# Alternating the order of TensorE's threads by array tile in the recurrence stage of a two-block network

## The reference, cut to what matters

```
for d in range(2):        # RWKV-7 branch: 16 heads of 64, state (64, 64) per head
    S_t = S_{t-1} diag(w_t) - (S_{t-1} kk_t) b_t^T + v_t k_t^T;   y_t = S_t r_t
for d in range(2):        # gated delta rule: 8 heads of 128, state (128, 128) per head
    a_mat = I + strict_lower(kb k^T * decay)          # one per chunk of 64 tokens
    u, w  = solve(a_mat, [v * beta, kb * exp(gc)])
    v_new = u - w S;  o = (q exp(gc)) S + attn v_new;  S = S * g_end + k_end^T v_new
```

## Time and profile before

| what | us |
|---|---|
| median of 3 runs | 3913.81 |
| lowest, highest | 3911.79, 3920.32 |
| span of the profiled execution | 3908.8 |
| stage B in it, first to last matmul | 985 |

### The profile page before, as it was taken

One profiled execution on the slowest core, in us unless ns is written; L12 is line 12 of the kernel. 1 busy time (PEld: TensorE's weight loads), 2 busy tenths in 40 slices (PEclk: granted clock), 3 DMA queues, 4 the chain that ended last, 5 costly groups with the idle time before them and its releaser, 6 DMA issues. The chain is left out here.

```text
span 3908.8 us, 85968 instructions
## 1 busy us (share of the span) xinstructions
PE 3701.0 (95%) x37216; PEld 3426.5 (88%) x37216; DVE 2097.1 (54%) x3808; ACT 1503.6 (38%) x2641; POOL 1661.9 (43%) x1195
## 2 busy tenths in 40 slices
PE   7899998899998999999979999999998999999998
PEld 6799988799997788888868888888888999999998
DVE  5435434434435776677766666666646553434343
ACT  4344434334444432332223333333334444435343
POOL 4455555455554553333321111111115566666664
PEclk9999998999999999999989999999998999999999
DMA  5355553345444777778610010000006545555553
GB/s 214 128 184 186 192 185 141 140 173 184 162 162 147 251 264 263 246 253 293 222 38 20 24 27 28 19 15 23 6 3 232 178 173 185 182 184 183 184 184 130
DMA packets 116392, 587.21 MB, mean 150 GB/s; under 512 B 20912, under 2 KB 40496, under 8 KB 51376
## 3 DMA queue, kind: packets, MB, share of 16 engines
q1 hardware_dynamic: 116016, 581.71, 41.9%
HBM read 560.95 MB, written 20.71 MB: 149 GB/s over the span
## 5 line engine op out<-in xcount | busy, mean ns | idle before, releaser
L556 PE MATMUL bank<-act_L,part_L 128*128 128x256 f32 x7296 | 958.9, 290 | 10.4 <-DMA cst<-in_cst 4.7
L556 PEld LDWEIGHTS bank<-act_L,part_L 128*128 128x128 f32 x7296 | 913.6, 196 | 48.0 <-issue 28.4
L3023 POOL TENSOR_TENSOR part_L<-wring,part_L 128x512 fp32r<-128x512 f32 x304 | 533.3, 1755 | 550.7 <-ACT part_L L1329 550.7
L556 PE MATMUL bank<-act_P,part_P 128*128 128x512 f32 (+1 forms) x3488 | 716.2, 365 | 17.7 <-POOL part_P L3023 12.9
L3023 POOL TENSOR_TENSOR part_C<-wring,part_C 128x512 fp32r<-128x512 f32 x320 | 569.6, 1789 | 368.9 <-ACT part_C L1329 368.9
L556 PEld LDWEIGHTS bank<-act_P,part_P 128*128 128x128 f32 x3488 | 590.3, 188 | 136.9 <-DVE arena_P L2447 16.1
L556 PE MATMUL bank<-arena_B 64*64 64x64 f32 (+2 forms) x11200 | 542.4, 230 | 38.9 <-DVE arena_B L2560 21.1
L556 PEld LDWEIGHTS bank<-arena_B 64*64 64x64 f32 (+2 forms) x11200 | 479.4, 142 | 88.9 <-DVE arena_B L2560 23.4
L3023 POOL TENSOR_TENSOR part_P<-wring,part_P 128x512 fp32r<-128x512 f32 x184 | 306.0, 1669 | 427.7 <-ACT part_P L1329 427.7
L2048 DVE TENSOR_TENSOR part_L<-wring,part_L 128x512 fp32r<-128x512 f32 x304 | 241.2, 795 | 445.3 <-ACT part_L L1329 445.1
L1329 ACT ACTIVATE part_C<-wring 128x1024 fp32r<-128x1024 f32 x320 | 337.9, 1057 | 360.9 <-PE bank L556 357.9
(11 more groups left out here) (250 smaller groups left out, 3430.2 us busy)
## 6 DMA issues: line engine op xcount, KB each, us to landing
wring<-in_w SPq DMA_DIRECT2D x404, 1024.0 KB, 4.8
arena_P<-in_w SPq DMA_DIRECT2D x64, 1024.0 KB, 5.1
mring<-in_w SPq DMA_DIRECT2D x32, 1024.0 KB, 6.4
z_kept<-arena_P SPq DMA_DIRECT2D x34, 256.0 KB, 5.6
z_kept<-arena_P SPq DMA_DIRECT2D x58, 128.0 KB, 5.9
xT<-z_kept SPq DMA_DIRECT2D x26, 256.0 KB, 2.8
arena_C<-z_kept SPq DMA_DIRECT2D x32, 128.0 KB, 3.0
cst<-z_kept SPq DMA_DIRECT2D x24, 128.0 KB, 2.1
```

What stands on the lines that cost most here:

```text
L556: return e.matmul(out, lhsT, rhs, start=start, stop=stop)
L3023: e.tensor_tensor(wl[:, 4:8, :], wring[s % NS][:, 8 * j + 4:8 * j + 8, :], wh[:, 4:8, :].bitcast(F32), sub).then_inc(*mark("pool_lo", "lop ...
```

## The change

`Weave` gets a second way to run streams, used by the four engines in stage B alone. What a stream yields is now a hint: 64 if its next step begins with 64x64 matmuls, nothing otherwise. In a turn, TensorE first advances the threads of one kind and then those of the other, each kind in the old order, and the kind that comes first alternates: large, small; then small, large; then large, small. On the other three engines nothing yields a hint, so their order within a turn stays. On all four, `until` looks in a copy of the set taken at the start of the turn, so a word is seen in the turn after it was said.

```diff
     def __init__(self):
-        self.said = set()
+        self.said, self.seen = set(), None
+
+    def run_grouped(self, *streams):
+
+        left, small = [(s, None) for s in streams], False
+        while left:
+            self.seen = set(self.said)
+            first = [x for x in left if (x[1] == 64) == small]
+            turn, order = first + [x for x in left if (x[1] == 64) != small], {}
+            for s, _ in turn:
+                hint = next(s, "end")
+                if hint != "end":
+                    order[id(s)] = hint
+            if any((x[1] == 64) != small for x in left):
+                small = not small
+            left = [(s, order[id(s)]) for s, _ in left if id(s) in order]
+        self.seen = None
...
     def after(self, n, word, stream):
 
-        for i, _ in enumerate(stream):
-            yield
+        for i, hint in enumerate(stream):
+            yield hint
...
     def until(self, *what):
-        while not all(x in self.said for x in what):
+        while not all(x in (self.said if self.seen is None else self.seen) for x in what):
             yield
```

On TensorE the six `yield` statements that come before a step of `inverse` become `yield 64` (four in `inverse` itself, which stand for twelve turns, the last one of `scores`, and the one after kq in `thread_b`). The four calls for stage B become:

```diff
-            weave.run(thread_a(0), thread_b(0), thread_a(1), thread_b(1), tail_a(), tail_b(), base_a(), base_b())
+            weave.run_grouped(thread_a(0), thread_b(0), thread_a(1), thread_b(1), tail_a(), tail_b(), base_a(), base_b())
```

More of the change, by code:

```diff
@@ L1002, in inverse @@
                 diagonal(bank(), NA, None, True).then_inc(*mark("pe_inv", "iq", tag, 0))
-                yield
+                yield 64
                 for lv in range(1, 6):
```

## The result

The changed kernel takes **4076.6 us** (median of 4 runs, 4074.8 to 4084.4) beside 3912.8 for the kernel before on the same chip: ratio 1.0422, 95% interval 1.041 to 1.0435. The direction was forecast, the size was not: +164 us against +29, outside the range.

A forecast was written before the change was run, and what follows sets the result against it. TensorE's own rate was taken to bound the kernel while results return before each thread's next turn. Terms -41 + 78 - 12 + 4 = +29 us gave 3943 us; 8-in-10 range 3882 to 3985, its own range 3925 to 3965.

The forecast's parts named there:

- Changes of tile: Stage B on TensorE: switches between 64x64 and other tiles fall from 500 to about 260, at 0.17 each, -41 us.
- Waits for a norm's power: Stage B, spreads of tails and bases: small steps now lie between sums and spread, removing some 12 of 15.7 us.
- Boundary waits: Stage B turn boundaries with the same kind on both sides: results not back, 10.4 us per head, +78 us.
- thread_a's cr: Chain steps at large|large boundaries: cr after ch waits +0.67 beside b's chain, 0.85 with nothing between.
- b's alone at the last levels: Small|small boundaries, last levels of b's inverse: a wait of 0.6 us, twice per head.
- The tail's ymean to sums: RWKV tail at a large|large boundary: TensorE waits 1.2 us per head between ymean and sums.
- The order of the other engines: VectorE and ScalarE queues in stage B: unalternated order may block TensorE, up to some 88 us; taken as 0.
- The words: Ends of stage B: words seen a turn later add about 3 turns of 1 to 2 us, +4 us.
- The clock: Body of stage B: clock at 0.99 of full speed, 2.4 GHz; no term for it in the sum.
- Rival 3: Blocking behind the other engines' fixed order: half of 88 us on top of the sum, 3987 us, chance 0.14.
- Rival 1: Waits at same-kind turn boundaries overlap and are absorbed: 2.5 us per head left, faster at 3884 us, chance 0.24.
- What would show it wrong: Signs: stage under 977 us, TensorE idle up by less than 40 us, or VectorE rows late after finished matmuls.

The follow-up runs named there:

- large-first run: Against the changed kernel, TensorE takes large steps first and small second in every turn, never alternating; other engines keep their order: 4278.5 us, ratio 1.0939.
- alternation alone: Against the kernel before, only TensorE's order within a turn alternates by kind, with every step in its old turn: 4085.7 us, ratio 1.0438.
- words with phases kept: Against the kernel before, words are seen a turn later with counts shortened, so only tails move, one turn late; TensorE's order is old: 3935.3 us, ratio 1.0063.

## Why the prediction was wrong, by its own steps

- *Changes of tile, 500 to about 260, -41 us.* Right in number: 268, so -232 x 0.17 = -39 by the prices of the earlier trace rows, and the spacings of 0.20 and 0.15 us at a change come back in the changed kernel. But no run isolates the saving, and it can't be read from the busy time (see the clock, below).
- *Waits for a norm's power, -12.* Right: 15.7 to 3.4 us.
- *Boundary waits, +78, 10.4 per head.* Idle ahead of steps rose by 236 - 98 = 138, and as 12 of the norms' waits went, the boundaries cost 150, about twice the term. The places listed were mostly the right ones and the chain's prices held: thread_a's cr waits 0.66 to 0.94 per place (forecast 0.67 and 0.85), b's alone at the last levels 0.57 twice (0.6). The failed terms are the tails and bases. The tail's ymean to sums was priced with 1.2 and is 3.46; base_b's sums (2.80), ymean (1.49) and vt (1.33) were not in the list at all. Together they are 25.5 + 21.6 + 10.4 + 9.3 = 67 us of idle, 58 of the missing 72 above the 1.2 x 7.5 = 9 that I had. They were missed because I listed threads against threads at boundaries and did not follow the four other streams, which carry no hint and so go with the large ones.
- *The order of the other engines, taken as 0.* The wrong choice, and together with the tails and bases the step that failed: the large-first run loses 366 us with the distances kept but in one place, with VectorE idle 4.14 us at another thread's copy while the tail's input is ready; and base_b's wait of 2.63 us goes when all engines follow. The 63 us of putting tails and bases last are order and distance together. In the close-ups of the tail and of kq VectorE or ScalarE serves another thread's part of the same turn first. I set it to nothing because "it costs nothing where the copy was due anyway"; that would hold only if a thread's copies were the first in the queue. The rule of the Trainium skill that I weighed (TensorE: Matmul & The Clock Gate, Architectural detail, engine queue depths), strict FIFO on ACT and DVE, is what the timelines show: L2772 behind L2565 and L2574, 2.0 us late. How much of the whole is order and how much distance I can't split exactly, as one makes the other worse.
- *The words, +4.* Wrong by itself: +45 under the old order. In the changed kernel it doesn't show in the sum, since alternation alone is as slow. It does show in the place: idle ahead of tail_a's sums is 3.19 us with the tail a turn late, beside thread_a's preparation, and 2.01 in the kernel of pure alternation.
- *The clock.* Not in the sum and not among the rivals. At 0.99 in the body I took the level as given. It is part of what is traded: +48.7 us of busy time for the same matmuls. 132 us more at 1.2 GHz bring 48.7; the two kernels in which only waits were moved or filled give 24.3 for 57 us and 24.1 for 88. The Trainium skill (TensorE: Matmul & The Clock Gate, Terms) puts the penalty at the time spent at the lower ratio times one half. By that rule, as an estimate, 132 us cost 66. The rows of this case lie under it, 0.27 to 0.43 of that time. A part of the low stretches is the wait itself: TensorE is busy in them for 139 us of 178 in the changed kernel and 39 of 46 before, and half of the difference, 50, is close to 48.7. That leaves nearly no room for a saving of 39 in the busy time. Some of it is covered by the starts of waits, which count as busy: the changed kernel has 204 gaps over 0.15 us instead of 64, at some 0.16 each 22 us, and the other reading of idle is larger by as much (138 instead of 117.5). How much of the 39 was really had stays open.
- *The rivals.* Rival 3 named the mechanism, at half of its upper end, 3987 us; even the whole 88 us on top of my sum (4031) would have been 46 us short; waits that lower the clock as well are in neither. Rival 1 (waits absorbed) had 0.24 and nothing for it: the waits at sums recur to 0.01 us in seven heads. What would show it wrong, "VectorE rows start late with their matmuls long done", is what the close-up of kq shows. The stated range ends, 3882 and 3985, are each 2 us under the middles of rivals 1 and 3 that they are taken from (3884, 3987); it changes nothing.
- The stage was forecast at 1014 us from 985; from its first matmul it is 1151.

So of the 166 us: 117.5 are time not busy, and 48.7 more busy time, from the lower clock and the starts of more waits, net of what the changes of tile save.

## What to carry to other kernels

An order in which one engine alone is rearranged has to be checked against the queues of the engines that serve it: for each step ask what stands ahead of its result there, in the tail and base streams as well, and not only how far it is from the thread's last step. A busy TensorE pays an idle stretch twice, once for the wait and again behind it at 1.2 GHz, so waits of 2 to 3 us can cost more than their length: filling 43.9 us of them took 24.1 us off the other matmuls. A saving per step of 0.17 us is no match for waits of a microsecond that come back in every head.

## What was not expected of the hardware

- Two kernels with the same instructions and within 1.3 us the same time not busy differ by 25.6 us in the stage, 24.3 of them busy time (before, and words with phases kept: the tails stand one turn later, and the idle time lies elsewhere).
- 201 matmuls of no use, 44.0 us of work, made the changed kernel 17 us faster by the medians, and the intervals of the two ratios don't touch.
- A wait doesn't always lower the clock: the kernel before has a wait of 1.58 us at thread_a(0)'s iq in 7 heads, and the clock fell at 2 of them; with words a turn late and phases kept it fell at 6 of the same 7. The sum of the idle time doesn't tell whether it falls.
